# The first modulation group in two halves by feature, with two input projection units between them

## The reference

```python
m = jax.nn.silu(cond) @ w + b            # _adaln, w_mod[0] is 1024 x 6144
sh1, sc1, gt1, sh2, sc2, gt2 = split(m, 6)
h = rmsnorm(x) * g * (1 + sc1) + sh1     # _modulate
proj = h @ w_in                          # 1024 x 3600: attention q,k,v, DeltaNet q,k,v, z, gates
```

## Time and profile before

| | |
|---|---|
| median of 3 runs | 1379.74 us (1378.78 to 1380.05) |
| the profiled execution | 1380.04 us |
| its span, first to last instruction | 1378.3 us |
| TensorE busy | 1338.7 us (97%) |
| VectorE / ScalarE / GpSimd busy | 400.3 / 282.4 / 108.3 us |
| moved by DMA | 499.86 MB, mean 363 GB/s |

### The profile page before, as it was taken

How to read it: one execution, slowest core, us unless ns; L and a number is a source line. 1 busy time by engine, 2 the same in 40 slices (tenths; PEclk the granted TensorE clock), 3 DMA queues, 4 the chain that set the end, 5 groups by cost and what they waited for, 6 DMA issues and landing times.

```text
span 1378.3 us, 23298 instructions
## 1 busy us (share of the span) xinstructions
PE 1338.7 (97%) x10242; PEld 705.6 (51%) x10242; DVE 400.3 (29%) x517; ACT 282.4 (20%) x364; POOL 108.3 (8%) x182
## 2 busy tenths in 40 slices
PE   4999999999999999999999999999999999999987
PEld 2997677678888885333333333333333333333332
DVE  2856344666444454101201400401101100100213
ACT  2673534453344333000000000000000000000011
POOL 6200141324000001000000000000000000010010
PEclk9999999999999999999999999999999999999998
DMA  9854967988777779999999999999999999999995
GB/s 382 306 161 152 379 252 277 405 311 301 244 244 245 260 293 416 363 360 427 427 423 430 427 422 412 424 410 430 424 426 429 425 425 427 428 423 427 425 428 239
DMA packets 103750, 499.86 MB, mean 363 GB/s; under 512 B 10514, under 2 KB 14303, under 8 KB 74855
## 3 DMA queue, kind: packets, MB, share of 16 engines
q1 hardware_dynamic: 87664, 471.75, 84.7%
q10 hardware_dynamic: 13590, 18.29, 3.7%
q0 software_dynamic: 2400, 8.42, 1.5%
HBM read 478.74 MB, written 19.69 MB: 362 GB/s over the span
## 4 chain that ended last, share of the span: by engine, by line
PE 92%; DMA 4%; DVE 2%; ACT 1%; issue 1%; ACTq 0%; DVEq 0%; SPq 0%
PE ps L2523 21%; PE ps L2520 17%; PE ps L2550 15%; PE ps L458 5%; PE ps L460 5%; PE ps L459 5%; PE ps L2557 4%; DMA ring_a<-in_moe_down 3%; PE ps L1927 3%; PE ps L1913 2%; PE ps L2059 1%; PE ps L2060 1%; PE ps L2061 1%; PE ps L2203 1%; PE ps L2016 1%; DMA raw<-in_w_mod 1%
## 5 line engine op out<-in xcount | busy, mean ns | idle before, releaser
L399 DVE TENSOR_TENSOR w_lo<-raw,w_hi 128x2048 fp32r<-128x2048 f32 x60 | 144.8, 2416 | 124.2 <-ACT w_hi L395 124.2
L2523 PE MATMUL ps<-ring_a,hTf 128*32 128x512 f32 (+1 forms) x1488 | 146.7, 551 | 0.0
L395 ACT ACTIVATE w_hi<-raw 128x2048 fp32r<-128x2048 f32 x59 | 112.8, 1914 | 108.7 <-PE ps L460 99.8
L2520 PE MATMUL ps<-raw,hTf 128*64 128x512 f32 (+1 forms) x624 | 123.8, 552 | 0.9 <-DMA raw<-in_moe_up 0.9
L1862 DVE TENSOR_TENSOR hm<-gate_bc,ps 32x384 f32<-32x384 f32 (+1 forms) x56 | 34.0, 607 | 267.5 <-PE ps L2520 266.6
L1868 DVE TENSOR_TENSOR hm<-gate_bc,ps 128x384 f32<-128x384 f32 (+1 forms) x16 | 9.4, 588 | 345.5 <-PE ps L2523 345.3
L2523 PEld LDWEIGHTS ps<-ring_a,hTf 128*32 128x32 f32 x1488 | 47.9, 110 | 96.9 <-issue 93.9
L458 PE MATMUL ps<-w_hi,hTh 128*128 128x512 f32 x232 | 91.5, 394 | 0.0
L460 PE MATMUL ps<-w_lo,hTh 128*128 128x512 f32 x232 | 90.4, 389 | 0.0
L459 PE MATMUL ps<-w_hi,hTl 128*128 128x512 f32 x232 | 90.3, 389 | 0.0
L2520 PEld LDWEIGHTS ps<-raw,hTf 128*64 128x64 f32 x624 | 44.1, 137 | 78.0 <-issue 74.9
(11 more groups left out here) (429 smaller groups left out, 1776.1 us busy)
## 6 DMA issues: line engine op xcount, KB each, us to landing
raw<-in_w_mod SPq DMA_DIRECT2D x48, 1024.0 KB, 7.8
raw<-in_moe_down SPq DMA_DIRECT2D x22, 2048.0 KB, 22.6
ring_a<-in_moe_down SPq DMA_DIRECT2D x20, 2048.0 KB, 19.1
ring_a<-in_moe_up SPq DMA_DIRECT2D x14, 2048.0 KB, 18.8
raw<-in_moe_gate SPq DMA_DIRECT2D x13, 2048.0 KB, 18.3
ring_b<-in_moe_down SPq DMA_DIRECT2D x13, 2048.0 KB, 19.5
ring_a<-in_moe_gate SPq DMA_DIRECT2D x11, 2048.0 KB, 24.6
raw<-in_moe_up SPq DMA_DIRECT2D x10, 2048.0 KB, 15.5
```

The lines of the kernel that those rows point to most:

```text
L395: nc.scalar.activation(w_hi[:, w % SPLIT], raw[:, slot % RAW], ACT.Copy).then_inc(s["hi_ready"], 1)
L399: nc.vector.tensor_tensor(w_lo[:, w % SPLIT], raw[:, slot % RAW], w_hi[:, w % SPLIT].bitcast(F32), ALU.subtract).then_inc(s["lo_ready"], 1)
L2520: last = MM(ps[HB * j:HB * j + HB, part % 4, 0:w], xT[:, kt, HB * (g // 2):HB * (g // 2) + HB], wt[:, kt % 2, 2 * (g % 2) + j, :], start=k ...
L2523: last = MM(ps[TOK * j:TOK * j + TOK, part % 4, 0:w], xT[:, KT * g + kt], wt[:, kt % 2, j, :], start=kt == 0, stop=kt == KT - 1)
```

## The change

Group 0's units are cut the other way. A unit now holds four input blocks (512 inputs) by 512 output columns (2 KB in a row of memory). Units 0 to 3 make the shift and scale of features 0 to 511 (half 0), units 4 to 7 those of features 512 to 1023. Two projection units of half 0 (of the first and of the second chunk) are loaded between the halves. TensorE's order becomes: product 0, the transposes of the small vectors, products 1 and 2, the transposes of `xn0` and of the first half's shift, product 3, the transposes of the half's scale; the eight unused matmuls; unit 0 whole; products 4, 5, 6; unit 1's high x high; product 7; unit 1's other terms with the second half's transposes between them; then units 2 and 3 (half 1 of both chunks) with the gate products behind them. Each product accumulates over two units only, in a bank of its own for shift and scale.

```diff
-ORDER = (mods(0) + splits(0, WOUT + 2) + ...
+ORDER = (mods(0)[:HALF] + splits(0, 2) + mods(0)[HALF:] + splits(2, WOUT + 2) + ...
+WIN_HALVES = ((0, 0), (1, 0), (0, 1), (1, 1), *((i, h) for i in range(2, 7) for h in range(2)))
...
+                if g == 0:
+                    h, u = i // HALF, i % HALF
+                    load_unit(sp, ("mod", i), rows(w_mod[0], 4 * (u % 2), D * (u // 2) + 512 * h))
...
+            mod_load(0)
+            fetch(x[:, 0], x_prompt[0], "x_loaded")
+            fetch(x[:, 1], x_sample[0], "x_loaded")
+            for i in range(1, HALF):
                 mod_load(i)
+            for n in range(2):
+                win_load(n)
+            for i in range(HALF, MOD_KT):
+                mod_load(i)
...
     GpSimd: fold_ab ahead of tri; unit 0 ahead of lev; unit 2 in the middle of lev
+            unit_high(0)
             step(nc.gpsimd.memset(lev[:, :, :, :], 0.0))
             for l in range(LEVELS):
+                if l == 3:
+                    pool.wait_ge(s["hi_ready"], 2)
+                    unit_high(2)
...
     ScalarE
             norm(0)
-            copy_rows(0, 0)
-            act.wait_ge(s["scp_ready"], 1)
+            copy_half(0)
             modulate_half(0)
+            act.wait_ge(s["hi_ready"], 1)
+            unit_hi(act, 1)
+            copy_half(1)
             modulate_half(1)
-            act.wait_ge(s["hi_ready"], 1)
+            act.wait_ge(s["hi_ready"], 3)
...
     VectorE
             norm(0)
+            save_half(0)
             modulate_half(0)
             low_half(0)
             unit_lo(dve, 0)
+            unit_lo(dve, 1)
+            save_half(1)
+            modulate_half(1)
             low_half(1)
+            unit_lo(dve, 2)
+            unit_lo(dve, 3)
+            unit_lo(dve, 4)
...
     TensorE
+            pe.wait_ge(s["c_loaded"], 32)
+            turn(ps[:, 1, 0:16], rowsA[0:16, :], 16).then_inc(s["rows_turned"], 1)
...
+            first_product(0)
+            turn_vectors()
+            for i in range(1, HALF):
+                first_product(i)
+                if i == 2:
+                    turn_first()
+                    turn_half(0, 0)
+            turn_half(0, 1)
             for i in range(8):
-                MM(ps[:, 3, 0:256], ident[:, :], flat(cstat), start=True, stop=True)
+                MM(ps[:, 0, 0:256], ident[:, :], flat(cstat), start=True, stop=True)
+            term_hh(0)
+            term_hl(0)
+            term_lh(0)
+            for i in range(HALF, MOD_KT - 1):
+                first_product(i)
+            term_hh(1)
+            first_product(MOD_KT - 1)
+            turn_half(1, 0)
+            term_hl(1)
+            turn_half(1, 1)
+            term_lh(1)
+            for n in (2, 3):
+                term_hh(n)
+                term_hl(n)
+                term_lh(n)
+                if n == 2:
+                    pe.wait_ge(s["mod_cols_saved"], 1)
+                    mix_gates()
+                else:
+                    fold_gates()
```

More of the change, by code:

```diff
@@ L692, in _, with unit_high @@
             pool.sem_inc(s["consts_ready"], 1)
[L694 to L697, removed]
+            def unit_high(i):
+                n = AT["split", i]
+                pool.wait_ge(raw_full[n % RAW], 16 * (n // RAW + 1))
+                nc.gpsimd.tensor_copy(w_hi[:, i % SPLIT], raw[:, n % RAW]).then_inc(s["hi_ready"], 1)
             step(nc.gpsimd.memset(rev[:, :], 0.0))
@@ L949, in modulate, with copy_half @@
                         .then_inc(s["h_hi_ready"], 1)
+            def copy_half(h):
+                for w in range(2):
+                    act.wait_ge(s["mod_used"], HALF * h + 2 * w + 2)
+                    nc.scalar.activation(mrow_first[:, h, w], ps[:, 2 + w, :], ACT.Copy).then_inc(s["mod_rows_copied"], 1)
             def modulate_half(h):
                 act.wait_ge(s["xn_turned"], 2)
+                act.wait_ge(s["scp_ready"], h + 1)
                 for t in range(4 * h, 4 * h + 4):
-                    last = nc.scalar.activation(hTf0[:, t, P:2 * P], ps[:, 6 + h, (t % 4) * P:(t % 4 + 1) * P],
+                    last = nc.scalar.activation(hTf0[:, t, P:2 * P], ps[:, 5 + 2 * h, (t % 4) * P:(t % 4 + 1) * P],
                                                 ACT.Identity, scale=scp[:, 0, t, 1:2], bias=mcol[:, 0, t, 1:2])
@@ L2008, in spread_lengths @@
                         last.then_inc(s["len_turned"], 1)
-            def first_chunk(h):
-                def term(w, x, start, stop):
-                    for q in range(4):
-                        for t in range(4):
-                            kt = 4 * h + t
-                            last = MM(ps[:, q // 2, (q % 2) * 256:(q % 2 + 1) * 256], w[:, h, t, q * P:q * P + P], x[:, kt, :],
-                                      start=start and kt == 0 and q % 2 == 0, stop=stop and kt == KT - 1 and q % 2 == 1)
-                    return last
-                pe.wait_ge(s["hi_ready"], h + 1)
-                pe.wait_ge(s["h_hi_ready"], h + 1)
-                term(w_hi, hTh0, True, False)
-                pe.wait_ge(s["h_lo_ready"], h + 1)
-                term(w_hi, hTl0, False, False)
-                pe.wait_ge(s["lo_ready"], h + 1)
-                term(w_lo, hTh0, False, True).then_inc(s["weights_used"], 1)
@@ L2028, in _, with chunk_term @@
-            for i in range(8):
-                MM(ps[:, 3, 0:256], ident[:, :], flat(cstat), start=True, stop=True)
-            pe.wait_ge(s["mod_cols_saved"], 1)
-            for i, (kind, _) in enumerate(WIN_ORDER):
+            def chunk_term(n, w, xT):
+                i, h = WIN_HALVES[n]
+                first, last_one = h == 0 and w is w_hi and xT is hTh0, h == 1 and w is w_lo
+                for q in range(4):
+                    for t in range(4):
+                        last = MM(ps[:, 4 * i + q // 2, (q % 2) * 256:(q % 2 + 1) * 256], w[:, n % SPLIT, t, q * P:q * P + P],
+                                  xT[:, 4 * h + t, :], start=first and t == 0 and q % 2 == 0, stop=last_one and t == 3 and q % 2 == 1)
+                return last
@@ L2042, in _ @@
                             spread_lengths()
-                        continue
-                    if i == 0:
-                        first_chunk(h)
-                        if h == 0:
-                            mix_gates()
-                        else:
-                            fold_gates()
                         continue
```

182 lines of the change are left out of this document (106 added, 76 removed).

## The result

The changed kernel takes 1382.28 us (median of 20 runs, 1379.79 to 1389.28), the kernel before beside it 1379.45 (20 runs, 1378.13 to 1382.87). The ratio is 1.0019, interval 1.0013 to 1.0026: slower by 0.19%, where a gain of 3.5 us was forecast and 1380.0 was the upper end of the range.

What follows compares the result with a forecast made beforehand. TensorE bounds the middle and releases the expert stream that bounds the end. Start at 24.2 plus 31.75 ends `fold_gates` at 55.95 instead of 59.45, 3.5 us earlier: 1376.5, for the median 1376.2; range 1373.8 to 1380.0.

Steps and rivals of the forecast that it cites:

- In the new order TensorE has gaps before 13.6 and works without one from there: TensorE's start: unbroken work from 13.6 us, so the clock goes to its high level and stays there.
- I take 2.5: Sixteen transposes after product 2: 1.97 us at the high level, twice that at the low one, put down as 2.5.
- the 3.6 for the unused matmuls: Eight unused matmuls just before the first projection matmul: 3.6 us, done at 24.2.
- turn_half: Transposes of the modulation sums: first some 0.4 us, second 0.66, the two of the second half 1.0 together.
- unused matmuls of over 4 us: Sign named beforehand that the forecast is wrong, at the eight unused matmuls before the first projection matmul.
- Rows of 2 KB: Loads of the modulation units: shorter rows could land 0.1 us a MB slower; nothing taken, up to 0.5 us in the range.
- no collision at either half: `scp` just misses GpSimd's rounding: 0.2 us at half 0, a 1 us margin at half 1; rival of a collision there, 0.18.
- the stall before unit 2: TensorE waits for half 1's tokens: 3.3 us of chain under a 1.95 us term, 1.35 idle, 1.6 with VectorE's wait.
- the arrival of the shift at the end: A microsecond won before 60 us reaches the kernel's end undiminished: 3.5 us earlier in all later stages.
- GpSimd's rounding of unit 2: After the masks, which wait 5.8 us for VectorE's subtractions, it runs 36.2 to 38.1 us, ahead of half 1's `scp` at 39.
- The rival with the unused matmuls at the low level: Half pace from 13.6 us, unused matmuls 7.2 us, first term at 30.9; 3.2 us slower, 1383; chance 0.08.
- the clock rival: TensorE's clock stays low longer, start at 25.2 to 26.4 us, gain of only 1.3 to 2.5 us; chance 0.15.

Runs made afterwards that it cites:

- keep_busy: The changed kernel with 18 more unused matmuls in TensorE's early gaps; ratio 0.9989 against the kernel before, median 1378.32 us.
- mod_rows_2k: The kernel before with group 0's eight units loaded in rows of 2 KB, its order kept; ratio 0.9999 against the kernel before.
- before_no_collision: The kernel before with GpSimd's rounding of unit 0 held back until `scp` is made; ratio 0.9983 against the kernel before.
- after_again: The changed kernel, unedited, measured once more; ratio 1.0020 against the kernel before.
- after_unused32: The changed kernel with its eight unused matmuls cut into 32 of 64 columns; ratio 1.0088 against the kernel before.
- before_unused32: The kernel before with its eight unused matmuls cut into 32 of 64 columns; ratio 1.0024 against the unedited kernel before.

## Why the prediction was wrong, by its own steps

**The step that failed** is "In the new order TensorE has gaps before 13.6 and works without one from there", and with it "I take 2.5" for the transposes and the 3.6 for the unused matmuls. From one start to the next, forecast and measured: landing of unit 2 13.6 and 14.31 (+0.7); product 2 1.7 and 1.87 (+0.2); transposes 2.5 and 3.46 (+1.0); first `turn_half` 0.4 and 1.33 (+0.9); product 3 1.07 and 1.06; copy 0.65 and 0.81 (+0.2); second `turn_half` 0.65 and 0.89 (+0.2); unused matmuls 3.6 and 5.03 (+1.4). That is the 4.6 us from 24.2 to 28.76. keep_busy, with the level high, has 1.00 for the product, 1.80 for the transposes, 0.89 and 0.88 for the two `turn_half`, 3.55 for the unused matmuls, and a start of 24.71. What the runs showed in its place: I gave the level one change, upward, at a time read from one execution. It changed twice, and at other times in other executions. The sign "unused matmuls of over 4 us", which I had named, came true with 5.39. There was a gap, too: I had costed the copy's hand-over at 0.65 and still called the work unbroken.

**`turn_half`** was mis-sized. I priced it by four transposes, 0.5; it is eight records, 0.9. Over four of them that is 1.5 us, of which 0.7 lies between 28.76 and 61.65. That stretch took 32.9 in place of 31.75; the rest, 0.4, is spread over units 0 and 1 in pieces of under 0.2.

**Rows of 2 KB** cost some 0.6 of the 0.7 us by which unit 2 was late. I took nothing and kept 0.5 for the range; mod_rows_2k has 397 GB/s against 422.

**Right** were: no collision at either half; the stall before unit 2, 1.41 against 1.6, and its cause; no wait of TensorE for `w_lo` or for a projection unit; the arrival of the shift at the end. **Right by luck** was GpSimd's rounding of unit 2 at 36.2 to 38.1. I had the masks end at 36.2 and the data there from 34.6; the masks ended at 35.18 and the rounding then waited 1.03 us for its unit ([1.03 <-DMA raw<-in_w_in] above), which landed 1.6 us later than forecast. Why it landed late stays open; the slot, free at 30.57 in place of 28, is not the reason, for in keep_busy it was free at 28.09 and the unit's rounding started at 36.49. The rival with the unused matmuls at the low level, to which I gave 0.08, described the way: its last `turn_half` at 23.7 was 23.86. It put the start at 30.9; it came at 28.76, and the loss there is 2.2 us. With the clock rival it was 0.23 together. I argued against both from the three gaps of the earlier trace rows over which the level held. That was one execution's luck and no property of such gaps: the same order with the same kind of gaps lost the level at 23.1 us in before_no_collision (behind waits of 1.17 and 1.79 us) and at 19.5 in mod_rows_2k (behind 0.74 and 1.47).

**The size of the loss.** Of 3.9 us in the spans, 2.2 are there at 61.65 us. Of the others, 0.7 are idle times without a named cause, 0.4 each the waits at 215 and 265 us, and 0.2 come behind 527 us. The profile is of an execution of 1383.91 us, 1.6 above the median, so the 2.2 us is one execution's share, not the median's. In after_again (1382.35 us, near its median) the start was 26.21 and `fold_gates` no later than before; of its 2.3 us in the spans none is there at 60 us, 0.9 at the tile `fold`, and 1.4 come behind it, where nothing was tried. Behind the tile `fold` the spans of all these profiles go on for 850.3 to 854.0 us, so a single profile can't place such a loss.

The executions' own mean granted clocks are on record, and the times go with them. Of the changed kernel's 31 executions (this run and after_again) the 6 with a mean of 0.995 took 1386.3 us on average and the 10 with 0.998 took 1381.2. The kernel before's 121 executions beside the experiments took 1381.3 (12 at 0.995) and 1379.7 (48 at 0.998). So a low clock goes with 5 us in the changed kernel and with 1.6 in the kernel before; but at 0.998 the changed one is still 1.5 us slower. The low level before 20 us is not in these means, since the granted clock reads 1.00 there.

That the level decides the start is shown: all five profiles with the 16 early fillers have the transposes at 1.97 us and a start of 24.2 to 24.7, and the seven without them 2.48 to 3.68 us and, with the eight unused matmuls as they were, 26.2 to 28.8. That it explains all of the median's loss is only argued; what supports it is that keep_busy, with no other edit, turned 1.002 into 0.9989.

**Open**: what TensorE waits for in those idle times between 157 and 212 us (0.8 to 3.1 us in sum in every profile, before too, but that of after_unused32, which has none), and why the level rises and falls at other times in executions of one kernel.

## What to carry to other kernels

When an early stage is pulled forward into a stretch where TensorE has little work, price every step at both clock levels, and look at more than one profile before you fix the time of a change of level: a fall that cost 1.4 us stood in two of the seven profiles that had the same 0.81 us gap, and not in the others. A kernel whose TensorE waits for landings hides a low level, and the change that removes the landing exposes it; here 18 filler matmuls in groups of 2 to 8 turned a loss of 0.2% into a gain of 0.1%, and a better order for half 1 made it 0.16 to 0.25%. When you take an oddity such as the 1.81 us of `scp` along with a larger change, try its removal alone first: it was worth about as much. Count float32 matmuls by records, two for each, not by columns, when they are narrow.

## What the runs showed of the hardware that I had not expected

In after_unused32 TensorE was busy with 64-column matmuls for 13.00 of 13.00 us and stayed at a granted clock of 0.50 from 24 to 37 us, and on through the first term with 256 columns (3.62 for 16 records). In before_unused32 the same matmuls began at the high level and kept it: 7.00 of 7.00 us busy from 29 to 36 us, at 1.00. The Trainium skill ("TensorE: Matmul & The Clock Gate", Part 1) says that activity releases the throttle. In the first of these stretches 13 us of full busy share went by without a release.

The level fell with only short idle times ahead of it: at 24.0 us behind one of 0.81 (the changed kernel), at 23.1 behind 1.17 and 1.79 (before_no_collision), at 19.5 behind 0.74 and 1.47 (mod_rows_2k). Behind the first of these it held in after_again, and behind the second in the kernel before.

The granted clock reads 1.00 at the start of the changed kernel's profile though the pace is half: 1.93 us for a product at 7, 11 and 14 us, 1.06 at 20.97. The kernel before has the same: 1.00 from 8 to 14 us (the first line under mod_rows_2k), and 5.78 us for 32 records at 12.07 in the earlier trace rows. The durations have to be read there.

Narrow float32 matmuls gained nothing from being narrow: at the high level 64 records of 64 columns took 7.26 us, 0.113 each, and the eight records of a `turn_half`, with 2 columns, 0.9. Sixteen records of 256, with the same columns as the 64, took 3.62.
